# Two fused transformer stacks: column sums of the modulation ahead of outputs, a fourth weight tile in halves, the result stored in four parts

## What is computed

```
first stack, layer i: mod = silu(c) @ w_mod[i] + b_mod[i]      # 6 x 1024 values: shift, scale, gate, twice
    x = x + g1 * mixer(modulate(x))                            # layer 0: latent attention (MLA), layer 1: short convolution
    x = x + g2 * experts(modulate(x))                          # 32 experts of 1024 x 512, gate, up, down
second stack, layer l: x = layer_norm(a * x + 0.5 * ffn1(x))
    x = layer_norm(a * x + mixer(x))                           # window attention and retention
    x = layer_norm(a * x + 0.5 * ffn2(x))
```

## Time and profile before

| | us |
|---|---|
| runs | 2303.36, 2311.8, 2312.47 |
| median | 2311.8 |
| the profiled execution | 2304.18 |
| its span in the trace | 2302.4 |

### The profile page before, as it was taken

The page is one execution under the profiler, slowest core; times in us unless marked ns, Lnnn a source line. Parts: engine busy times, 40 slices in busy tenths (PEclk is TensorE's granted clock), DMA queues, the critical chain, the costliest instruction groups (busy, mean ns, idle before and its releaser), DMA issues.

```text
span 2302.4 us, 45938 instructions
## 1 busy us (share of the span) xinstructions
PE 2019.7 (88%) x18008; PEld 1553.8 (67%) x18011; DVE 1193.6 (52%) x2420; ACT 802.4 (35%) x1566; POOL 27.0 (1%) x40
## 2 busy tenths in 40 slices
PE   7999888676779988676777999998999999998997
PEld 3557655343449955344446888887888888887886
DVE  3777322111227632111125766768667766768765
ACT  2233211000015411000003654556555654556654
POOL 0000000000000000000000000100001000100001
PEclk9999999888989999888898999999999999999999
DMA  9978899999997699999999656344556546334551
GB/s 393 369 285 345 355 431 431 431 432 432 431 424 302 242 405 430 431 432 431 432 431 352 213 155 204 110 136 137 193 151 208 183 145 208 123 109 150 200 155 49
DMA packets 271556, 660.36 MB, mean 287 GB/s; under 512 B 6336, under 2 KB 198864, under 8 KB 246352
## 3 DMA queue, kind: packets, MB, share of 16 engines
q1 hardware_dynamic: 270976, 656.72, 73.4%
q10 hardware_dynamic: 464, 2.05, 0.2%
HBM read 657.69 MB, written 1.06 MB: 286 GB/s over the span
## 4 chain that ended last, share of the span: by engine, by line
PE 65%; DMA 19%; DVE 7%; SPq 3%; issue 2%; ACT 2%; another core or an unknown queue 1%; DVEq 0%; ACTq 0%; PEldq 0%
PE ps L2470 19%; DMA A<-in_moe_w_up 10%; PE ps L2475 10%; PE ps L1830 7%; DMA ring<-in_moe_w_up 6%; PE ps L2811 4%; PE ps L1859 3%; SPq L3376 2%; DMA arena<-in_moe_w_up 2%; PE ps L1812 2%; PE ps L2255 1%; PE ps L1780 1%; PE ps L2257 1%; PE ps L2256 1%; PE ps L2852 1%
## 5 line engine op out<-in xcount | busy, mean ns | idle before, releaser
L2470 PE MATMUL ps<-XS,WS 128*128 128x512 f32 x1280 | 451.7, 397 | 8.1 <-DVE WS L2451 8.0
L2451 DVE TENSOR_TENSOR WS<-ring,WS 128x1024 fp32r<-128x1024 f32 (+1 forms) x272 | 324.3, 1194 | 179.7 <-ACT WS L2446 179.3
L2446 ACT CAST WS<-ring 128x1024 fp32r<-128x1024 f32 (+1 forms) x272 | 278.3, 1024 | 269.0 <-PE ps L2475 264.7
L2475 PE MATMUL ps<-XS,WS 128*128 128x256 f32 x1280 | 359.2, 281 | 0.0
L2112 DVE TENSOR_TENSOR RS<-RS,ps 64x256 f32<-64x256 f32 x70 | 29.6, 423 | 571.7 <-ACT RS L1919 571.7
L1830 PE MATMUL ps<-ring,RS 128*32 128x256 f32 x2176 | 237.5, 448 | 86.8 <-DMA ring<-in_moe_w_up 33.8
L2470 PEld LDWEIGHTS ps<-XS,WS 128*128 128x128 f32 x1280 | 240.2, 188 | 68.7 <-issue 5.9
L2475 PEld LDWEIGHTS ps<-XS,WS 128*128 128x128 f32 x1280 | 241.8, 189 | 0.0
L1830 PEld LDWEIGHTS ps<-ring,RS 128*32 128x32 f32 x2176 | 124.7, 128 | 152.8 <-issue 132.2
L2470 PE MATMUL ps<-HS,WS 128*128 128x512 f32 x616 | 216.8, 397 | 0.0
L1830 PE MATMUL ps<-arena,RS 128*32 128x256 f32 x1120 | 165.6, 461 | 50.7 <-DMA A<-in_moe_w_up 23.4
(11 more groups left out here) (405 smaller groups left out, 3527.6 us busy)
## 6 DMA issues: line engine op xcount, KB each, us to landing
ring<-in_ffn_w_gu SPq DMA_DIRECT2D x88, 1024.0 KB, 7.2
arena<-in_moe_w_down SPq DMA_DIRECT2D x32, 2048.0 KB, 47.7
ring<-in_moe_w_up SPq DMA_DIRECT2D x32, 2048.0 KB, 46.3
ring<-in_moe_w_down SPq DMA_DIRECT2D x32, 2048.0 KB, 46.7
ring<-in_moe_w_gate SPq DMA_DIRECT2D x32, 2048.0 KB, 45.8
ring<-in_w_mod SPq DMA_DIRECT2D x24, 2048.0 KB, 11.8
ring<-in_ffn_w_down SPq DMA_DIRECT2D x32, 1408.0 KB, 6.5
SPARE<-in_moe_w_gate SPq DMA_DIRECT2D x16, 2048.0 KB, 43.2
```

The source lines that it names most:

```text
L2446: L.inc(L.eng.copy(self.parts(u)[0], source), self.w_high)
L2451: L.inc(L.eng.tensor_tensor(wl, self.unit(u)[1], high(wh), ALU.subtract), self.w_split)
L2470: L.eng.matmul(ps[:, bank, :].rearrange("p (j t) -> p j t", j=2), wh[:, i, :], moving[:, :, k, :], start=k == 0, stop=False)
L2475: mm = L.eng.matmul(ps[:, bank, 0:TL], wl[:, i, :], moving[:, 0, k, :], start=False, stop=k == total - 1)
```

## The change

It has five parts.

- **Sums ahead of outputs.** In each attention unit `sum_rows(u+5)` stands ahead of `outputs(u)`, and ScalarE's `keep_sums` ahead of `copy_outputs` (and, in odd units, of the next exponentials). The sums of tiles 5 to 12 go to bank 0 or 2, the unit's own scores bank, and `scores` waits for their copy.
- **Opening.** MLAC is loaded behind mla_w_dkv, and its readers wait for it where they use it. Turns 0 and 1 stand behind the products of tiles 0 and 1, two `keep_busy` products follow, and turn 2 stands ahead of the wait for tile 3.
- **Halved fourth tile.** Tile 3 comes in two DMAs of 1 MB, and `stream_weights` goes through the row blocks in order, so that the first half of the products needs the first half of the tile alone. The second half's semaphore is `mix_in`, whose later readers wait for 32 in place of 16.
- **Last norm.** In the last turn VectorE subtracts the mean from tile 7 between variance and root; GpSimd leaves it out.
- **Store.** Four DMAs of two tiles each, issued as `done` counts them.

```diff
@@ -151,7 +151,7 @@
 DVE_PER_LAYER = 173
-DVE_LAST = 169
+DVE_LAST = 170
 SPLITS_PER_LAYER = 2 * FFN_UNITS + MIXER_UNITS
@@ -268,6 +268,7 @@
         mix_in = sig("mix_in")
+        second_half = mix_in
         stages_done = sig("stages_done")
@@ -381,6 +382,9 @@
                     plan(columns(w["w_mod"][0], 512 * s, 512 * (s + 1)), (KD, 512), (self.rows, s + 1), s)
+                dst, src = loads[self.first + 3].pop()
+                loads[self.first + 3].append((dst[:, 0:4, :], src[:, 0:4, :]))
+                self.half = (dst[:, 4:KD, :], src[:, 4:KD, :])
@@ -401,15 +405,18 @@
                 L.eng.wait_ge(self.cond.sem, 2)
-                for s in range(self.SLOTS):
+                for s in range(2):
                     slot_ready(L, self.first + s)
-                    if s >= 2:
-                        L.eng.wait_ge(self.rows_kept.sem, s - 1)
-
-                    stream_weights(L, self.weights(s), 1 + s % 2, self.rows)
-                    if s:
-                        turn_rows(s - 1)
-                turn_rows(self.SLOTS - 1)
+                    stream_weights(L, self.weights(s), 1 + s, self.rows)
+                turn_rows(0)
+                turn_rows(1)
+                keep_busy(L, 2, 3)
+                slot_ready(L, self.first + 2)
+                stream_weights(L, self.weights(2), 1, self.rows)
+                turn_rows(2)
+                slot_ready(L, self.first + 3)
+                stream_weights(L, self.weights(3), 2, self.rows, second_half)
+                turn_rows(3)
                 end(L, "pe")
@@ -464,11 +471,13 @@
-        def stream_weights(L, weights, bank, signal):
+        def stream_weights(L, weights, bank, signal, half_in=None):
             for i in range(4):
+                if i == 2 and half_in:
+                    L.eng.wait_ge(half_in.sem, 16)
                 for j in range(4):
-                    k, c = 4 * (j // 2) + i, j % 2
+                    k, c = 2 * i + j // 2, j % 2
                     mm = L.eng.matmul(ps[32 * j:32 * (j + 1), bank, 0:TL], COND[:, k, :], weights[:, k, c * TL:(c + 1) * TL],
@@ -552,7 +561,9 @@
-                return (5, slice(0, P)) if j < 13 else (6, slice(SUMS_AT, SUMS_AT + P))
+                if j >= 13:
+                    return 6, slice(SUMS_AT, SUMS_AT + P)
+                return 5 if j < 5 else (j - 5) % 2 * 2, slice(0, P)
@@ -660,8 +671,12 @@
+            def own_tiles(self, L):
+
+                return () if not self.raw or self.goes_on(L) else (KD - 1,)
+
             def pe_centre(self, L):
-                L.eng.wait_ge(mix_in.sem, 16)
+                L.eng.wait_ge(mix_in.sem, 32)
                 L.wait(self.ready, 1)
@@ -755,6 +770,10 @@
                                                  op0=ALU.add, op1=ALU.subtract), self.var)
+                own = self.own_tiles(L)
+                for k in own:
+                    L.wait(self.kept, 3)
+                    L.inc(L.eng.tensor_tensor(LN_OFF[:, k, :], LN_OFF[:, k, :], LN_MEAN, ALU.subtract))
                 L.wait(self.std, 1)
@@ -763,7 +782,8 @@
                 for k in range(KD):
-                    L.wait(self.less_mean, k + 1)
+                    if k not in own:
+                        L.wait(self.less_mean, k + 1)
                     L.inc(L.eng.scalar_tensor_tensor(out=XT[:, k, 0:TL], in0=LN_OFF[:, k, :],
@@ -785,6 +805,8 @@
                 for k in range(KD):
+                    if k in self.own_tiles(L):
+                        continue
                     d = LN_OFF[:, k, :]
@@ -1196,7 +1218,6 @@
                 pe, later = L.eng, self.later
-                pe.wait_ge(mla_in.sem, 16)
@@ -1240,6 +1261,7 @@
                 later.turn_rows(L, 0)
+                pe.wait_ge(mla_in.sem, 16)
                 L.inc(pe.matmul(ps[0:ROPE, 4, 0:TL], TURN[0:ROPE, 0:ROPE], QRAW[0:ROPE, :], start=True, stop=True), self.kpe_turned)
@@ -1305,6 +1327,7 @@
                         L.eng.wait_ge(self.exps.sem, 2 * (u - 1))
+                        L.wait(later.sums_kept, u + 4)
                     for j in range(2):
@@ -1316,7 +1339,8 @@
                         L.eng.wait_ge(self.turned_copied.sem, 2 * u)
-                    L.wait(later.sums_kept, u + 5)
+                    if u == 0:
+                        L.wait(later.sums_kept, 5)
                     for j in range(2):
@@ -1350,6 +1374,7 @@
                     later.turn(L, u + 4)
+                    later.sum_rows(L, u + 5)
@@ -1372,6 +1397,7 @@
                         L.eng.wait_ge(self.exps.sem, 14)
+                        L.wait(later.sums_kept, 12)
                         output_tile(1, range(6))
@@ -1380,7 +1406,6 @@
                     outputs(u)
-                    later.sum_rows(L, u + 5)
@@ -1481,13 +1506,13 @@
                         copy_rope(p + 1)
+                    self.later.keep_sums(L, u + 5)
                     copy_outputs(u)
-                    self.later.keep_sums(L, u + 5)
                     copy_turned(u + 1)
+                    self.later.keep_sums(L, u + 6)
                     if p + 1 < self.PAIRS:
...
                     copy_outputs(u + 1)
-                    self.later.keep_sums(L, u + 6)
                 for m in range(KD):
@@ -1502,7 +1527,6 @@
                 dve, later = L.eng, self.later
-                dve.wait_ge(mla_in.sem, 16)
@@ -1525,6 +1549,7 @@
                     r = slice(0, ROPE)
+                    L.eng.wait_ge(mla_in.sem, 16)
                     L.eng.wait_ge(self.kpe_turned.sem, 1)
@@ -3148,7 +3173,7 @@
                 begin(L, "dve")
-                v.wait_ge(mix_in.sem, 16)
+                v.wait_ge(mix_in.sem, 32)
@@ -3328,14 +3353,16 @@
             sp.dma_start(XT[:, :, :], xT).then_inc(x_in.sem, 16)
-            sp.dma_start(MLAC, mla_c).then_inc(mla_in.sem, 16)
-
             def load(n):
...
                     sp.dma_start(dst, src).then_inc(slot_in[place_of[n]].sem, 16)
+                if n == opening.first + opening.SLOTS - 1:
+                    sp.dma_start(*opening.half).then_inc(second_half.sem, 16)
+                if n == mla.dkv:
+                    sp.dma_start(MLAC, mla_c).then_inc(mla_in.sem, 16)
@@ -3388,9 +3415,12 @@
+            last_norm = lns[2]
+            for k in range(0, KD, 2):
+                sp.wait_ge(last_norm.done.sem, last_norm.done.base + (LAYERS - 1) * last_norm.done.per_turn + k + 2)
+                sp.dma_start(out[:, k:k + 2, :], XT[:, k:k + 2, 0:TL]).then_inc(const_in.sem, 16)
             sp.wait_ge(stages_done.sem, 3 * (len(first_stack) + 1 + LAYERS * len(layer)))
-            sp.dma_start(out, XT[:, :, 0:TL]).then_inc(const_in.sem, 16)
-            sp.wait_ge(const_in.sem, 48)
+            sp.wait_ge(const_in.sem, 32 + 16 * KD // 2)
...
         def _(pool):
```

## The result

| us | before | changed |
|---|---|---|
| median (7 runs each) | 2307.22 | 2295.68 |
| lowest to highest | 2303.36 to 2312.47 | 2291.04 to 2299.37 |
| the profiled execution | 2304.18 | 2299.37 |
| its span | 2302.4 | 2297.6 |

The ratio is 0.9949, with a 95% interval of 0.9936 to 0.9962: 11.8 us faster. Forecast were 3.9. The two profiled executions differ by only 4.8: that of before is near the lowest of its kernel's seven, that of after is the highest.

The account below looks back on a forecast made before the run. Bound mostly by TensorE products (65% of the chain), and by the weight stream in the expert stages. +1.4 -1.8 -1.2 -2.0 -0.3 = -3.9 us, off the median 2311.8, gave 2307.9; range 2295.5 to 2311.

Parts of the forecast that it names:

- the low level of 2303.8: Range's lower end: a median of a few runs may fall on the level of 2303 to 2304, instead of 2311.8.
- the opening's gain carried: Rival, opening: first later tile lands sooner, TensorE keeps 3 us and doesn't idle; -8.4 in all, 2303.4; chance 0.08.
- Opening: +1.4: Before the first sums: 0.1 of 3 us gained is left, and a clock fall after idling costs +1.5.
- the fall behind the wait: Clock falls after TensorE idles before 52.5 us, +1.5; forecast 0.55, rival without a fall (-5.4, 2306.4) 0.20.
- Units 2 and 4 have no such gap: 0: Attention units 2 and 4: the query turn stands where other units wait, so moving the sums saves 0.
- units 1, 3, 5 and 6: Attention: outputs no longer wait 0.21 us for ScalarE's copy; each unit saves 0.3, together -1.2.
- unit 0: Attention: sums ahead of outputs let VectorE go on sooner, ending TensorE's wait for the rotation; -1.8.
- The sums wait for VectorE: Rival, each attention unit: sum_rows finds its tile unfinished; +12, with the rest +6 or so, 2318; chance 0.04.
- End, -2.3: Last norm and store: the store in four parts gives -2.0, the subtraction moved to VectorE -0.3.
- The tail: Store: 4.96 us from issue to span end shrinks since the last of four parts takes 0.7 us; -2.0.
- the subtraction on VectorE: Last norm: GpSimd ends 0.75 sooner, but the subtraction makes the reciprocal 0.4 late; net -0.3, bounds +0.4 and -0.5.
- The base: Whole kernel: the gain was subtracted from 2311.8, the median of runs at 2303.36, 2311.8 and 2312.47.

Follow-up runs that it names:

- e10: Changed kernel with sum_rows(0) behind the key tile's products and two added keep_busy products, timed against the kernel before: ratio 0.9941, median 2294.12 us.
- e11: Changed kernel with the first later tile loaded ahead of mla_w_dq and two added keep_busy products, timed against the kernel before: ratio 0.9940, median 2294.99 us.
- e9: The changed kernel again, unedited, timed against the kernel before: ratio 0.9949, 11.8 us faster, median 2297.74 us.
- e3: Opening part alone (MLAC's place, turns, keep_busy, halved fourth tile) on the kernel before: ratio 0.9994, -1.4 us (-4.2 to +1.6).
- e7: Kernel before with sums ahead of outputs, except units 2 and 4, put back behind their outputs: a single execution, 2302.46 us.
- e4: End part alone (tile 7's subtraction on VectorE, store in four parts) on the kernel before: ratio 0.9996, 0.9 us faster.
- e5: Changed kernel with the first later tile of w_mod loaded ahead of mla_w_dq, timed against the kernel before: ratio 0.9943, median 2291.86 us.
- e6: Changed kernel with sum_rows(0) behind the key tile's products instead of ahead, timed against the kernel before: ratio 0.9939, median 2290.43 us.
- e1: The changed kernel again, unedited, timed against the kernel before: ratio 0.9963, 8.5 us faster.
- e8: Kernel before with keep_busy products added in its opening's idle times, against the kernel before: ratio 0.9991, 2.1 us faster.
- e2: Attention part alone (sums ahead of outputs) on the kernel before: ratio 0.9980, 4.6 us faster.

## Why the prediction was right or wrong

The measured 2295.68 lies inside the range (2295.5 to 2311) by 0.2 us, and by luck: that end stood for a median at the low level of 2303.8 and the opening's gain carried, and neither came. The change was faster as forecast, but by three times as much. Every place was named rightly; the sizes and one sign were off.

- **"Opening: +1.4"** is the step that failed. Its mechanism was in the trace after, to 0.1 us (idle 3.10, low clock, +1.3), and the loss of the gain at the first sums is shown by e10 and e11. But the base was one execution whose down products ran at full clock. In three of four traces of the old opening a low stretch went into them and past the sums; in the changed one what the products lose goes into the waiting time ahead of the sums, in e9 to the last of it (no idle time is left there). By the eight traces the term is **-1.7** on the first scores. The traces show how the loss is absorbed; the size and even the sign are less certain, since 1.7 is uncertain by about 1.0 (which leaves +1.4 three times that away) and the times don't fix it (e3 alone: -1.4, from -4.2 to +1.6). The text had asked what a fall costs the changed kernel, and not what the falls on rows 3 cost the old one where they last longer. It also took the fall behind the wait for the rule (0.55 against 0.20): it came in one trace of four.
- **"Units 2 and 4 have no such gap: 0"** failed: 0.42 each (e7). The query turn (L1300) waited 0.16 us for ScalarE's copy, so that there too the sums cost less in their new place than 0.36: L1295 to L1300 grew from 2.42 to 2.55. The other part is that outputs and scores each run 0.1 sooner without the sums between them (1.87 to 1.78, 2.98 to 2.87). The same 0.1 was missed elsewhere: unit 1, whose scores stand behind idle time in both kernels, gave 0.33 for the forecast 0.3, but units 3, 5 and 6, whose scores also run 0.1 sooner (2.97 to 2.87), 0.44 or 0.45 each. So units 1, 3, 5 and 6 gave 1.7 for 1.2, units 2 and 4 0.85 for 0, and unit 0, whose wait for the rotation went but for 0.16, 1.9 for 1.8. Together -4.4 for -3.0; timed alone 4.6 (2.3 to 7.1).
- **"The sums wait for VectorE"**, the slower rival: no such wait in any trace of the changed order at units 0 to 7. Its sum was off as well: 12 with the forecast's -3.9 is +8, not +6.
- **End, -2.3**: measured -2.9. The tail shrank by 2.4, not 2.0, and the subtraction on VectorE gave 0.5, not 0.3. By the rule of the Trainium skill (SBUF — State Buffer, "SBUF: two separate sides"), worked out in the prediction, the subtraction sits out GpSimd's tile first and takes 1.17 us in all, an estimate. The trace has 0.87 beside GpSimd, as in rows 11; in e4 it starts 0.48 behind GpSimd's start and takes 0.52, and the reciprocal is not held at all. Here the measurement decides.
- **The sum**: -1.7 -4.4 -2.9 = -9.0 us, ratio 0.9961, inside the intervals of all three timings of the changed kernel; their middles lie at 8.5 to 11.8. Of the 7.9 us between forecast and measured 3.1 are the opening's, 1.4 the attention's and 0.6 the end's. Whether the 2.8 that are left are real, no run here shows.
- **The base**: the median of the three runs at hand, 2311.8, was 4.6 above that of seven, so that the forecast of 2307.9 missed by more than the mechanisms did. The profiled execution was 3 below.

## What to carry to other kernels

Price a change of waits against several executions, not one: where a wait ends decides whether the next low clock stretch is paid or absorbed, so slack ahead of a fixed arrival is worth something even if the mean path is as long. Ahead of such an arrival, either move the waiting instruction behind the next independent work or bring the awaited transfer forward; e10 and e11 did each in one line. It took the keep_busy products too: without them e5 and e6 had the down products end too late for it to show. Work moved out from between two streams of products can give back more than its own duration: look at the start-to-start times on both sides, in the even cases too.

## What was unexpected of the hardware

**Products have two paces at the same granted clock.** In the first layer's first FFN two executions ran the same products at a different rate. A stretch of 100 us, of the trace before and then of e4, columns as in rows 2:

```profile
1300.00:1400.00 100.00, 100.00 (x568) 86.74 (x567) 65.71 (x99) 54.07 (x96) 0.00 (x0) 1.00 0.53 165
```

```profile
1300.00:1400.00 100.00, 100.00 (x579) 87.42 (x578) 66.80 (x102) 55.21 (x97) 0.00 (x0) 1.00 0.53 166
```

and the costliest group of either stretch (mean ns of one):

```profile
L2470 PE MATMUL ps<-XS,WS 128*128 128x512 f32 x213 | 75.3, 399 | 0.0
```

```profile
L2481 PE MATMUL ps<-XS,WS 128*128 128x512 f32 x217 | 75.3, 394 | 0.0
```

568 products against 579, 1.9%, with PE busy throughout and the clock at 1.00. From 1600 to 1700 us e4 has 568 too, so that it changes within an execution, from stage to stage. In the thirteen traces the counts of these stretches are always 567 to 569 or 578 to 579, never between. From the first to the last product of the first FFN it is 177.2 us in the kernel before (1260.3 to 1437.5) and 174.8 in e4 (1262.5 to 1437.3): 2.4 us, and there are four FFNs. That would make it a candidate for the 9 us by which the runs of one kernel differ. But the changed kernel has the same pattern in its three traces (579, 568 and 579, within one, from 1300, 1600 and 1800 us on), though after and e1 differ by 4.8 us, so it isn't what separates those two; the kernel before has 568 in all three stretches of its one trace. What sets the pace, and whether it goes with the kernel or with the execution, is open.

**Low clock stretches differ from run to run** under the same instructions. In the first 62 us the old opening has 6.8 us of them (twice), 13.7 and 17.1, the changed one 3.4 (three times) and 10.2, and there are none in e8, e10 and e11, where keep_busy products fill the idle times. The idle times differ too (2.31 to 4.18 us ahead of the old opening's fourth tile), but they don't decide it: after and e6 both wait 0.81 us for the second half of the tile, and the clock stays up in the one and is low for 6.8 us in the other. Ahead of the first scores all thirteen traces have 1.40 or 1.41 us of idle time; a low stretch of 3.4 us follows in e2, e5 and e9, and none in the other ten.
